# Prologue and two borders of an eight-layer transformer kernel on one core: tables loaded in parts, zero products on TensorE, three PSUM banks, a reordered gate chain

## The reference, cut to what matters

```python
def first_block(x, positions, weights):   # layers 1 to 4
    # mixer 1: gated delta rule (conv over 4 taps, silu, l2 norm, 64-token chunks)
    #   beta = sigmoid(b);  g = -exp(a_log) * softplus(a + dt_bias)
    # mixer 2: latent attention (MLA); both are followed by a SwiGLU
    return rms_norm(x, final_norm)
def second_block(x, positions, weights):  # layers 5 to 8
    h = rms_norm_2(x, attn_norm_2[0])     # mixer 3: differential attention (da_*)
    # x = x + attention(h); SwiGLU; mixer 4: sliding window attention; SwiGLU
```

## Time and profile before

| | us |
|---|---|
| median of three runs | 1464.05 |
| profiled execution, its own time | 1463.53 |
| its span, first to last instruction | 1461.9 |
| TensorE busy in the span | 1408.9 (96%) |
| VectorE busy | 925.6 (63%) |
| ScalarE busy | 727.9 (50%) |
| GpSimd busy | 19.7 (1%) |

### The profile page before, as it was taken

The page is one execution under the profiler, slowest core; times in us unless marked ns, Lnnn a source line. Parts: engine busy times, 40 slices in busy tenths (PEclk is TensorE's granted clock), DMA queues, the critical chain, the costliest instruction groups (busy, mean ns, idle before and its releaser), DMA issues.

```text
span 1461.9 us, 19760 instructions
## 1 busy us (share of the span) xinstructions
PE 1408.9 (96%) x7739; PEld 1199.3 (82%) x7739; DVE 925.6 (63%) x1629; ACT 727.9 (50%) x1246; POOL 19.7 (1%) x44
## 2 busy tenths in 40 slices
PE   6799999999999999999999999999999999999998
PEld 5799989888888888888888878778888877888887
DVE  6667777756655546747555489876554586665543
ACT  5554545444544445645444365745544465454441
POOL 3010000000000000000000000000000000000000
PEclk9999999999999999999999999999999997999999
DMA  9332423124566554516665545236555541365552
GB/s 268 87 87 59 116 59 115 59 72 142 180 184 187 187 183 148 187 60 202 187 187 187 187 147 183 75 116 201 180 187 191 163 145 58 115 192 184 187 187 87
DMA packets 168107, 216.59 MB, mean 148 GB/s; under 512 B 11009, under 2 KB 136272, under 8 KB 167888
## 3 DMA queue, kind: packets, MB, share of 16 engines
q1 hardware_dynamic: 166832, 213.03, 47.2%
q10 hardware_dynamic: 1184, 2.31, 0.4%
HBM read 214.26 MB, written 1.05 MB: 147 GB/s over the span
## 4 chain that ended last, share of the span: by engine, by line
PE 84%; DVE 10%; ACT 3%; DMA 1%; issue 1%; DVEq 0%; SPq 0%; ACTq 0%
PE psum L890 22%; PE psum L892 22%; PE psum L891 22%; PE psum L1090 4%; DVE w_low L639 3%; PE psum L1274 2%; PE psum L1082 2%; PE psum L1250 2%; PE psum L1096 2%; PE psum L1211 1%; DVE work L2256 1%; PE psum L1263 1%; PE psum L881 1%; PE psum L672 1%; DVE x L2044 1%
## 5 line engine op out<-in xcount | busy, mean ns | idle before, releaser
L639 DVE TENSOR_TENSOR w_low<-ring,w_high 128x1024 fp32r<-128x1024 f32 (+3 forms) x395 | 475.2, 1213 | 325.3 <-ACT w_high L625 323.6
L625 ACT ACTIVATE w_high<-ring 128x1024 fp32r<-128x1024 f32 (+3 forms) x395 | 411.2, 1048 | 446.9 <-PE psum L892 433.5
L890 PE MATMUL psum<-w_high,hT 128*128 128x512 f32 (+2 forms) x944 | 372.3, 394 | 0.6 <-DVE hT L2063 0.6
L892 PE MATMUL psum<-w_high,hT 128*128 128x512 f32 (+2 forms) x944 | 366.9, 389 | 0.0
L891 PE MATMUL psum<-w_low,hT 128*128 128x512 f32 (+2 forms) x944 | 366.1, 388 | 0.0
L890 PE MATMUL psum<-w_high,parts 128*128 128x512 f32 (+1 forms) x532 | 208.1, 391 | 0.4 <-DVE work L2599 0.4
L892 PEld LDWEIGHTS psum<-w_high,hT 128*128 128x128 f32 x944 | 177.6, 188 | 36.8
L890 PEld LDWEIGHTS psum<-w_high,hT 128*128 128x128 f32 x944 | 177.8, 188 | 34.7 <-DVE hT L2063 0.9
L892 PE MATMUL psum<-w_high,parts 128*128 128x512 f32 (+1 forms) x532 | 206.0, 387 | 0.0
L891 PE MATMUL psum<-w_low,parts 128*128 128x512 f32 (+1 forms) x532 | 205.8, 387 | 0.0
L891 PEld LDWEIGHTS psum<-w_low,hT 128*128 128x128 f32 x944 | 177.8, 188 | 34.1
(11 more groups left out here) (276 smaller groups left out, 1395.2 us busy)
## 6 DMA issues: line engine op xcount, KB each, us to landing
ring<-in_ffn_w_gate_up SPq DMA_DIRECT2D x176, 256.0 KB, 3.2
ring<-in_w_gate_up SPq DMA_DIRECT2D x176, 256.0 KB, 3.2
ring<-in_gdn_w_in SPq DMA_DIRECT2D x48, 512.0 KB, 3.9
ring<-in_ffn_w_down SPq DMA_DIRECT2D x44, 512.0 KB, 3.2
ring<-in_w_down SPq DMA_DIRECT2D x44, 512.0 KB, 3.2
ring<-in_da_w_qkv SPq DMA_DIRECT2D x24, 512.0 KB, 4.0
ring<-in_gdn_w_out SPq DMA_DIRECT2D x16, 512.0 KB, 3.3
ring<-in_mla_w_out SPq DMA_DIRECT2D x8, 512.0 KB, 3.9
```

The lines of the kernel that those rows point to most:

```text
L625: nc.scalar.activation(piece_slot(w_high, n), piece_slot(ring, n), ACT.Copy).then_inc(s.w_hi, 1)
L639: nc.vector.tensor_tensor(piece_slot(w_low, n), piece_slot(ring, n), piece_slot(w_high, n).bitcast(F32), ALU.subtract).then_inc(s.w_lo, 1)
L890: mm(out, lhs[0], rhs[0], start=start, stop=False)
L892: return mm(out, lhs[1], rhs[0], start=False, stop=stop)
```

## The change

1. **Tables in parts.** `gates_loaded`: the constants `cum`, `ones`, `incl` and the vectors that the gates and lambda need (final_norm moves to the end of the vectors); `angles_loaded`: inverse frequencies and positions; `levels_loaded`: the level masks, issued after the Ln of the gates; `late_loaded`: attention masks and all other vectors, issued after `silu(3)`. GpSimd now does the angles first and the level sums behind them.
2. **Zero products.** TensorE multiplies a block of zeros by itself (128 x 128, fp32) 20 times from the start and 4 times between the turned x and the first products.
3. **Three banks.** Tiles 0 to 6 rotate over banks 6, 7 and 5; tile i waits for `conv(i - 3)` (from tile 8 on for `conv(i - 2)`, as before). `products(0)` now waits for `conv(5)`, by `conv_done` 6.
4. **Gate chain.** ba rows are copied and turned before tile 1 rather than after it; lambda's sums come first; cumulated sums and `gate_rows` stand before tile 3 rather than after tile 4; the silus come after `gate_exp`; masks are turned between tiles 3 and 4; `conv(7)` stands before `first_level(0)`.
5. **Scales in two.** `key_scales` (without the square root) keeps the old place; `other_scales` (the Newton chain, `k_len`, `q_inv`) goes to the end: for group 0 behind `first_y(0)`, for later groups behind the group's last instruction.
6. **Border of mixer 3.** Plain x is turned; the gains of both norms are multiplied in one column; `xy` is formed after `turned_low`.
7. **End.** The last token tile is summed and stored in two halves.

```diff
+FIRST_VECTORS = VECTOR_AT["da_q_norm_2"][0]
...
+        def tile_bank(i):
+            return B[(6, 7, 5)[i % 3] if i < 7 else 6 + i % 2][:, 0:SEQ]
...
@@ tensor
-                src = xy if k == 5 else x
...
+            def last_halves(pr, src):
+                for h in range(2):
+                    for n in range(pr.pieces - TAIL, pr.pieces):
+                        w = landed(pe, pr.first + n)
+                        last = mm3(B[6 + h][:, :], [src(b, n, 1) for b in range(2)],
+                                   [w[b][:, 0, h * HALF:(h + 1) * HALF] for b in range(2)], n == 0, n == pr.nk - 1)
+                    last.then_inc(s.half_sum, 1)
...
-                if i >= 2:
-                    pe.wait_ge(s.conv_done, i - 1)
+                if i >= 3:
+                    pe.wait_ge(s.conv_done, i - 2 if i < 8 else i - 1)
...
+            def idle_products(n):
+                for _ in range(n):
+                    mm(B[7][:, 0:P], zeros, zeros, start=True, stop=True)
+            pe.wait_ge(s.seeded, 1)
+            idle_products(20)
...
             first_norm()
+            idle_products(4)
             pe.wait_ge(s.table_ready, 2)
             beta_and_gate()
             tile(0)
-            tile(1)
             pe.wait_ge(s.ba_copied, 1)
...
-            turned_masks()
-            for i in range(2, 5):
-                tile(i)
+            tile(1)
+            tile(2)
+            pe.wait_ge(s.gates_loaded, 32)
             pe.wait_ge(s.gl_ready, 1)
...
             gate_rows(0)
+            tile(3)
+            turned_masks()
+            tile(4)
             tile(5)
@@ scalar
-            act.dma_start(consts[:, P:N_CONST], a["consts"][:, P:N_CONST]).then_inc(s.consts_loaded, 16)
-            act.dma_start(vectors[:, :], a["vectors"].partition_broadcast(P)).then_inc(s.small_loaded, 16)
+            act.dma_start(consts[:, P:LEVEL_AT], a["consts"][:, P:LEVEL_AT]).then_inc(s.gates_loaded, 16)
+            act.dma_start(vectors[:, 0:FIRST_VECTORS], a["vectors"][0:FIRST_VECTORS].partition_broadcast(P)).then_inc(s.gates_loaded, 16)
+            act.dma_start(const("inv_freq"), a["consts"][:, N_CONST - 32:N_CONST]).then_inc(s.angles_loaded, 16)
...
+            act.wait_ge(s.gates_loaded, 32)
+            f(alog, alog, ACT.Exp)
+            act.wait_ge(s.lam_sums, 1)
+            f(lam[:, 0:2], lam[:, 0:2], ACT.Exp).then_inc(s.lam_ready, 1)
             split_high(act, a_ba + SPLIT)
-            tiles(0)
-            tiles(1)
-            tiles(2)
+            tap(0)
             act.wait_ge(s.ba_abs, 1)
...
             f(tmp32[1], tmp32[1], ACT.Ln, bias=ones[:, 0:1]).then_inc(s.ba_act, 1)
-            silu(0)
-            tiles(3)
-            tiles(4)
-            silu(1)
+            split_high(act, tile_piece[0] + SPLIT)
+            act.dma_start(const("level"), a["consts"][:, LEVEL_AT:MASKS_AT]).then_inc(s.levels_loaded, 16)
+            tiles(1)
+            tiles(2)
             act.wait_ge(s.gcum_ready, 1)
             gate_diff(0)
             gate_exp(0)
...
+            tiles(3)
+            silu(0)
+            tiles(4)
+            silu(1)
             tiles(5)
...
             silu(3)
+            act.dma_start(consts[:, MASKS_AT:N_CONST - 32], a["consts"][:, MASKS_AT:N_CONST - 32]).then_inc(s.late_loaded, 16)
+            act.dma_start(vectors[:, FIRST_VECTORS:], a["vectors"][FIRST_VECTORS:].partition_broadcast(P)).then_inc(s.late_loaded, 16)
@@ vector
+            def final_gains(t):
+                dve.wait_ge(s.late_loaded, 32)
+                dve.wait_ge(s.x_ready, 2 * TURN[5] + t + 1)
+                tt(xy[:, t, :], x[:, t, :], gfin, ALU.mult).then_inc(s.y_ready, 1)
...
                 turned_low(k, 0)
+                if k == 5:
+                    final_gains(0)
...
+            own(tt(both_gains, both_gains, gains[:, GAIN_AT["final_norm"]:GAIN_AT["final_norm"] + KC], ALU.mult))
...
-            scales(0)
+            tiles(4)
+            tiles(5)
+            key_scales(0)
             tiles(6)
             key_products(0)
+            conv(7)
             first_level(0)
-            tiles(7)
             first_y(0)
+            split_low(dve, tile_piece[7] + SPLIT)
+            other_scales(0)
...
                 if more:
-                    scales(g + 1)
+                    key_scales(g + 1)
                     key_products(g + 1)
...
                 tt(pairs(gd_o[g][:, 1, :]), pairs(g_r.rearrange("p h n -> p (h n)")), rq[1], ALU.mult).then_inc(s.g_end, 1)
+                if more:
+                    other_scales(g + 1)
@@ gpsimd
-            pool.wait_ge(s.consts_loaded, 16)
-            tt(doubled[:, :, 0, :], doubled[:, :, 0, :], doubled[:, :, 1, :], ALU.add).then_inc(s.steps_summed, 1)
-            pool.wait_ge(s.small_loaded, 16 * N_SMALL)
+            pool.wait_ge(s.angles_loaded, 32)
...
+            pool.wait_ge(s.levels_loaded, 16)
+            tt(doubled[:, :, 0, :], doubled[:, :, 0, :], doubled[:, :, 1, :], ALU.add).then_inc(s.steps_summed, 1)
+            pool.wait_ge(s.late_loaded, 32)
```

More of the change, by code:

```diff
@@ L126, in __init__ @@
         self.sums = sem("sums")
+        self.half_sum = sem("half_sum")
         self.tp_psum = sem("tp_psum")
@@ L521, in program @@
         seed = cell(32)
+        zeros = view(work, 4096, P)
         posf = cell(4)
@@ L975, in tile @@
                 for k in range(KC):
-                    last = mm3(B[6 + i % 2][:, 0:SEQ], [w[b][:, k, :] for b in range(2)],
+                    last = mm3(tile_bank(i), [w[b][:, k, :] for b in range(2)],
                                [hT[:, b, k, :] for b in range(2)], k == 0, k == KC - 1)
@@ L2286, in scales, with other_scales @@
                         own(last)
-                last.then_inc(s.scales_ready, 1)
+                last.then_inc(s.beta_ready, 1)
+            def other_scales(g):
+                u = g % 2
+                sums, y = kq_ssq[u], kq_root[u]
+                n_k = T * GA
+                own(root_of(y, sums))
+                own.wait()
+                own(tt(k_len[u], sums[:, 0:n_k], y[:, 0:n_k], ALU.mult))
+                ts(q_inv[u], y[:, n_k:2 * n_k], GD ** -0.5, None, ALU.mult).then_inc(s.scales_ready, 1)
             def beta_of(g, t):
@@ L2355, in outputs_low @@
                     stt(lo, pairs(B[bank + q][:, :]), gain("gdn_out_norm", 0), hi.bitcast(F32), ALU.mult, ALU.subtract).then_inc(s.og_lo, 1)
-            used(dve, a_ba)
-            v.tensor_copy(ba_rows[0:2 * VH, :], B[4][0:2 * VH, 0:SEQ]).then_inc(s.ba_copied, 1)
+            dve.wait_ge(s.gates_loaded, 32)
+            for n in range(2):
+                own(tt(lam_row[:, 128 * n:128 * n + 64], lam_row[:, 128 * n:128 * n + 64], lam_row[:, 128 * n + 64:128 * n + 128], ALU.mult))
+            own.wait()
+            for n in range(2):
+                last = v.reduce_sum(lam[:, n:n + 1], lam_row[:, 128 * n:128 * n + 64], AX_X)
+            last.then_inc(s.lam_sums, 1)
             split_low(dve, a_ba + SPLIT)
-            tiles(0)
-            tiles(1)
-            dve.wait_ge(s.small_loaded, 16 * N_SMALL)
-            dve.wait_ge(s.consts_loaded, 16)
             dve.wait_ge(s.ba_psum, 1)
@@ L2369, in _ @@
             stt(tmp32[1], tmp32[0], -1.0, tmp32[0], ALU.mult, ALU.max).then_inc(s.ba_abs, 1)
-            for n in range(2):
-                own(tt(lam_row[:, 128 * n:128 * n + 64], lam_row[:, 128 * n:128 * n + 64], lam_row[:, 128 * n + 64:128 * n + 128], ALU.mult))
-            own.wait()
-            for n in range(2):
-                last = v.reduce_sum(lam[:, n:n + 1], lam_row[:, 128 * n:128 * n + 64], AX_X)
-            last.then_inc(s.lam_sums, 1)
-            tiles(2)
-            dve.wait_ge(s.mask_psum, 1)
-            v.tensor_copy(const("level")[:, P:(1 + STEPS) * P], B[2][:, 0:STEPS * P]).then_inc(s.mask_ready, 1)
+            conv(0)
             dve.wait_ge(s.lam_ready, 1)
```

117 lines of the change are left out of this document (62 added, 55 removed).

## The result

| | kernel before | changed kernel |
|---|---|---|
| median of the runs shown | 1463.86 us (1463.63 to 1466.27, 4 runs) | 1455.79 us (1455.18 to 1457.11, 4 runs) |
| profiled execution, its span | 1463.53, 1461.9 us | 1455.18, 1453.4 us |
| first turn of group 0 (`turned_y`) | 67.99 us | 55.61 us |

Forecast were 7.8 us and a time of 1456.2. The total agrees better than its terms do.

The account below looks back on a forecast made before the run. TensorE works 96% of the span, so only its idle or lower-clock time can be won. 10.7 - 4.4 + 0.4 + 1.1 = 7.8 us gave 1455.7, plus 0.5 for the median 1456.2; 8 in 10 within 1451.5 to 1460.0.

Parts of the forecast that it names:

- The start, put at 10.7 us: Start and prologue up to the first group: it begins at 57.3 instead of 67.99, 10.7 us won, bounds 8.2 to 12.
- My bound: Prologue: if one of TensorE's two waits of about 2 us ends with the lower clock, up to 1.4 us less won.
- Borders, 4.4 us lost: Three group borders: the Newton chain ahead of the next group's first mask makes VectorE 1.46 us late each time.
- borders cost nothing: Rival at group borders: the mask comes late, but the products behind it make it up; 1451.8 us, chance 0.12.
- they cost the clock: Rival at group borders: products after TensorE's rest come at 1.2 GHz, 1.7 us each time; 1461.2 us, chance 0.07.
- Border of mixer 3, 0.4: Mixer 3's border: `xy` leaves the path to both turns, the time is mostly lent; TensorE gains 0.2 to 1.2, taken 0.4 us.
- The wait that I had placed at the last roped quarter: Behind mixer 3's border: TensorE would wait at the last roped quarter, where the time won earlier is given back.
- the sign that I had named: Profile sign at the mixer's border: turns would come 1.2 us after the sum.
- part 4: The prediction's section on mixer 3's border: `xy` (1.23 us) leaves the path to both turns; 0.4 us won.
- End, 1.1: Kernel's end: one half to add after the last product and smaller stores; 1.1 us won, bounds 0.6 and 1.25.
- the slower rival: Prologue: level sums later than 36 us delay all tiles, each us costing one; 1467 or more, chance 0.04.
- The third rival: Start: zero products fail, pieces land late (0.6, 1.1, 1.4 us less), half of VectorE's slack gone; 1459.5 us, chance 0.12.

Follow-up runs that it names:

- e10: The changed kernel run once more, unchanged, for a second trace; 1456.21 us.
- e11: The changed kernel with the tables fetched as in the kernel before, one DMA each for constants, vectors and positions; 1460.99 us, ratio 0.9968.
- e3: The changed kernel with tiles in two banks and the old wait for the conv two tiles earlier; 1456.12 us, ratio 0.9937.
- e2: The changed kernel without its 24 zero products; 1455.73 us, ratio 0.9933.
- e8: The kernel before run once more, unchanged, for a second trace; 1464.41 us.
- e6: The kernel before with only the Newton chain and its two products moved behind each group's last instruction, group 0 unchanged; 1471.21 us, ratio 1.0036.
- e12: e1 run once more, unchanged; 1450.77 us, ratio 0.9901.
- e1: The changed kernel with the Newton chain and its two products right behind the key scales again for groups 1 to 3; 1450.45 us, ratio 0.9896.
- e9: The changed kernel with the end as before: both halves added together, one 512 KB store per tile; 1457.36 us, ratio 0.9944.
- e7: e1 with a new order in the prologue, tile 3 ahead of the gates' sums and others moved, against the changed kernel; 1450.87 us, ratio 0.9896.
- e4: The changed kernel with all tables (2.09 MB) loaded at once at the start, in seven DMAs; 1463.04 us, ratio 0.9980.

## Why the prediction was right, and where its terms were off

**The start, put at 10.7 us: the first group at 57.3.** Measured 55.61, 12.4 us won in these traces, which is above the stated bounds of 8.2 to 12. VectorE's `hT` rows came at 11.93 and not 12.95, because the second tile of x landed 1.4 us earlier than in the trace I worked from; from `hT` to `turned_y` I had 44.35 us and the trace has 43.68. So the layout by durations was off by 0.7 us in 44, and what I took as fixed, the landing of x, was 1.0 us of the miss. In e10 it is 45.05 us from `hT` (11.80) to `turned_y` (56.85), so here too the layout is as near as two executions are to each other. Taken apart by the undone parts, in the start alone: tables 6.0 (e11), third bank 2.0 (e3), zeros 0.3 (e2), and the rest, some 4 us, is the new order of the chain and the landing of x together. Each is the difference of two traces, parts undone one by one need not add up, and what the order gives by itself wasn't tried. I had given the zeros and the earlier `hT` together 1.8 us at the end of `beta_and_gate` (17.1 instead of 18.9). That rested on the trace, in which products are 0.21 us apart until 18 us. This was that execution's own: in e8 and e6, which have no zeros either, they are 0.12 us apart from the first product behind the turns on, and in e2 too. The first product in the trace before, and in e8:

```profile
14.59 0.39 PE L890 MATMUL psum<-hT,w_high 128*32 128x256 f32 x1 [0.79 <-DVE hT L696]
```

```profile
13.81 0.28 PE L890 MATMUL psum<-hT,w_high 128*32 128x256 f32 x1 [1.11 <-DVE hT L696]
```

So one trace was taken for the rule; without zeros the clock came up by then in three traces of four. And the turns, which do get faster by the zeros, end under VectorE's gains and low halves, which last to 12.73 in the earlier trace rows.

**A step that was right by luck.** TensorE's wait of 1.95 us was followed by the lower clock, `gate_rows` took 3.66 us where e10 and e12 show 2.03 after waits of 1.64 and 2.01. My bound said up to 1.4 us for that. There it cost nothing: TensorE waits for `silu` at 41 us anyway, 1.25 us in that trace and 2.56 to 2.82 where `gate_rows` was short. But e10 has the lower clock behind this other wait, of 2.70 us, and its first group is 1.24 us later. That is what the bound was for, and it is met.

**Borders, 4.4 us lost.** Measured 1.42 to 1.43 us at each (4.65 or 4.66 less 3.23), 4.3; e1 and e6 confirm it from both sides. Of the rivals, that borders cost nothing is out; that they cost the clock five times over is out too, but the right part of it is that one or two stretches more came in seven of the nine traces with late masks, and in one (e7) of the five without. Each costs 1.2 to 1.4 us. With so few traces that is a hint and not shown; e9 and e3 have late masks and none. I forecast none, and this is the term that was missing: -1.3.

**Border of mixer 3, 0.4:** 0.5 by ten traces against four. TensorE, for the earlier trace rows:

```profile
842.20 1.09 PE L889 MATMUL psum<-consts,x 128*128 128x128 f32 x8 [1.46 <-DVE x L2080]
...
907.65 1.09 PE L679 MATMUL psum<-consts,arena 128*128 128x128 f32 x8
...
915.38 1.08 PE L1285 MATMUL psum<-consts,work 128*128 128x128 f32 x6 [0.91 <-ACT work L1659]
```

and the row of the kernel before that answers to the last:

```profile
922.80 1.08 PE L1263 MATMUL psum<-consts,work 128*128 128x128 f32 x6 [0.68 <-ACT work L1628]
```

Ahead of the border the changed kernel is 6.8 us early, at the second turn 8.25, at the last roped quarter 7.7, at the next turn of x 7.4: lent and mostly given back, as forecast. The wait that I had placed at the last roped quarter isn't in its row, though. With the two traces laid beside each other row by row, the lead goes in small steps: 8.25 us until the turn of one roped quarter, 8.0 from there (891.93), 7.8 from the next (898.46), 7.7 from the last (907.65), and 7.4 from the attention's turn at 915.38, where TensorE waits for ScalarE 0.91 us and not 0.68. VectorE's second sum starts at 840.86, right behind its two low halves, as in the earlier trace rows 847.86, and ends at 842.14. So the turn at 842.20 stands right behind the sum; the sign that I had named, turns 1.2 us after it, was wrong and doesn't fit my own part 4, in which `xy` leaves their path.

**End, 1.1:** 1.05, of which the add is 0.6:

```profile
1447.20 0.69 DVE L2151 TENSOR_TENSOR x<-psum,x 128x512 f32<-128x512 f32 x1 [1.43 <-PE psum L900]
1449.92 0.69 DVE L2151 TENSOR_TENSOR x<-psum,x 128x512 f32<-128x512 f32 x1 [2.03 <-PE psum L900]
```

```profile
out<-x SPq DMA_DIRECT2D x2, 256.0 KB, 2.0
```

and the store, 2.0 us from issue to landing where the earlier trace rows have 2.6, the rest.

**The sum.** 12.4 - 0.2 (the scales of group 0: from `turned_y` to the products 3.47 us instead of 3.23) - 4.3 - 1.3 + 0.5 + 1.05 = 8.1, against 8.5 in the spans; the 0.4 left over lie between 562 and 654 us, where the two traces of the kernel before differ by 0.2 and those of e1 and e12 by 0.4. So the total came out because a start that won 1.7 more paid for a stretch at the lower clock that cost 1.3. The masks, the slower rival, had 2 us of air: GpSimd had its sums at 32.0 and TensorE asked at 33.9. The third rival's 1459.5 wasn't the sum of its terms: the 3.1 us give 1459.3, and half of a gap of 2.7 on top some 1460.6.

**The mechanisms beside it.** The table loads behave as their rows say. The part that costs, the scales, is the one to undo: e1 and e12 beat both kernels, 1450.45 and 1450.77 us.

## What to carry to other kernels

A chain of small instructions that moves off one engine's busy stretch must be given a place where someone waits for something else, not one ahead of the instruction that everybody waits for: eleven rows of 0.2 us at three borders took back a third of what the start had won. When many parts of a change touch the start, cut the trace at the first instruction of the steady part and undo them one by one; each gap that a part closes may be covered by another engine, as the zeros' was. A state that a plan rests on, such as a lower clock at the start, should be looked for in a second trace of the same kernel first. And where differences of 1 us matter, cut each trace into segments: the medians couldn't tell the end's 1.05 us, the last 189 us of fourteen traces could.

## What the hardware showed that I had not expected

- TensorE's lower clock comes behind waits of one and the same length in some executions and not in others. Timeline of TensorE in the changed kernel and then in e9, at the same place and with the same wait:

```profile
255.73 1.59 PE L1104 MATMUL psum<-work 128*128 128x128 f32 x8 [1.15 <-DVE work L2515]
256.97 0.77 PE L898 MATMUL psum<-w_high,hT 128*128 128x512 f32 x1
...
259.68 0.42 PE L898 MATMUL psum<-w_high,hT 128*128 128x512 f32 x1
```

```profile
255.69 1.16 PE L1099 MATMUL psum<-work 128*128 128x128 f32 x8 [1.15 <-DVE work L2507]
256.60 0.48 PE L896 MATMUL psum<-w_high,hT 128*128 128x512 f32 x1
```

  The windows of 252 to 258 and 258 to 264 us show a granted clock of 0.86 in the changed kernel and 1.00 in e9. Inside the groups two traces of one kernel agreed in their places three times out of three, kernels that differ elsewhere didn't; in the start only one pair of the three agreed (the changed kernel has its stretch at 28 us, e10 at 42). What decides is open.
- Where the kernel before has its second tile of x at 7.1 to 7.9 us (three traces), the changed start has it at 6.2 to 6.6 in ten of eleven, and at 7.12 in one. Neither the zeros (e2) nor the tables (e11) make it so, and the engines' rows until then are nearly the same (VectorE has one small instruction more). The cause was not found.
- A DMA issue on ScalarE's queue takes 0.34 to 1.05 us of its time in e4, and seven in a row where the changed kernel has four moved a copy by 2.4 us.
